# Late modulation in pairs of sections with the ones held in the array, and attention heads whose DVE and PE work is reordered

## The reference

```
m_lat = jnp.split((s_lat @ mod_w[l] + mod_b[l])[:, None, :], 6, axis=-1)   # six sections of 1024 per layer
u = modulate(rmsnorm(h, norm_mix[l]), m_lat[0], m_lat[1])
...
qd = q * exp(b); kd = k * exp(-b); kr = k * exp(b_last - b)     # b: running sum of the log gates in a chunk
o_intra = (mask * (qd @ kd^T)) @ v;   ds = kr^T @ v
s = decay * s + ds                                               # state from chunk to chunk, in both directions
o = o_intra + qd @ s_before
o = o * rsqrt(mean(o*o) + EPS) * gain * silu(g)
hyena: x0 * (fftconv(v * x1) + skip * v * x1), each of x0, x1, v after a 3-tap convolution
```

## Time and profile before

| | us |
|---|---|
| median of 3 timed runs | 2494.81 (2491.34 to 2498.23) |
| profiled execution, its own time | 2485.07 |
| its span | 2483.2 |
| PE busy in the span | 2370.1 (95%) |
| DVE busy | 1147.8 (46%) |
| ACT busy | 363.1 (15%) |
| mean granted clock of TensorE | 0.985 |

### The profile page before, as it was taken

The page is one execution under the profiler, slowest core; times in us unless marked ns, Lnnn a source line. Parts: engine busy times, 40 slices in busy tenths (PEclk is TensorE's granted clock), DMA queues, the critical chain, the costliest instruction groups (busy, mean ns, idle before and its releaser), DMA issues.

```text
span 2483.2 us, 33406 instructions
## 1 busy us (share of the span) xinstructions
PE 2370.1 (95%) x14147; PEld 1038.7 (42%) x14148; DVE 1147.8 (46%) x2426; ACT 363.1 (15%) x654; POOL 293.3 (12%) x313
## 2 busy tenths in 40 slices
PE   7999999989999999999999899999999999999997
PEld 3455445454555533333233344444555333333333
DVE  4677377757845523332222643444454333322226
ACT  3210333321012100000000230000121000000002
POOL 2000000001000212212220000000002212221200
PEclk9999999999999999999999999999999999999999
DMA  9586000120170699999999611113107999999994
GB/s 344 199 284 219 26 26 26 51 77 34 68 296 26 251 376 400 402 395 413 404 411 383 220 35 50 51 34 116 46 34 281 383 405 399 413 403 411 399 377 195
DMA packets 140562, 581.41 MB, mean 234 GB/s; under 512 B 16788, under 2 KB 41672, under 8 KB 87800
## 3 DMA queue, kind: packets, MB, share of 16 engines
q1 hardware_dynamic: 120680, 534.87, 55.3%
q0 software_dynamic: 19648, 44.09, 4.8%
q10 hardware_dynamic: 80, 0.26, 0.0%
HBM read 550.74 MB, written 44.32 MB: 240 GB/s over the span
## 4 chain that ended last, share of the span: by engine, by line
PE 76%; DMA 12%; DVE 10%; issue 1%; ACT 1%; POOL 0%; SPq 0%; DVEq 0%; POOLq 0%
PE ps L1736 23%; PE ps L1896 11%; PE ps L1771 9%; PE ps L1616 9%; DMA arena<-in_ex_w_dram 8%; PE ps L1392 2%; PE ps L1848 2%; PE ps L1360 2%; PE ps L1408 2%; DVE arena L2172 2%; PE ps L1429 2%; DMA arena<-expert_rows 1%; PE ps L1531 1%; PE ps L1550 1%; PE ps L1870 1%
## 5 line engine op out<-in xcount | busy, mean ns | idle before, releaser
L1736 PE MATMUL ps<-arena 128*32 128x512 f32 x6144 | 679.3, 597 | 16.2 <-DMA arena<-in_ex_w_dram 16.1
L1736 PEld LDWEIGHTS ps<-arena 128*32 128x32 f32 x6144 | 198.2, 110 | 449.7 <-issue 448.0
L1771 PE MATMUL ps<-arena 128*32 128x512 f32 x3072 | 340.2, 594 | 12.5 <-DMA arena<-in_ex_w_dram 12.2
L1896 PE MATMUL ps<-arena 128*128 128x512 f32 x616 | 264.5, 592 | 0.0
L2548 DVE TENSOR_TENSOR arena<-arena,ps 128x512 f32<-128x512 f32 x48 | 52.5, 1093 | 456.4 <-PE ps L1736 456.4
L1616 PE MATMUL ps<-arena 128*128 128x512 f32 x512 | 229.4, 598 | 1.6 <-DVE arena L2324 1.6
L1771 PEld LDWEIGHTS ps<-arena 128*32 128x32 f32 x3072 | 106.5, 110 | 238.0 <-issue 238.0
L843 POOL DMA_INDIRECT arena<-normed_rows,arena x184 | 185.2, 1006 | 110.2 <-DVE arena L2566 53.9
L2593 DVE TENSOR_TENSOR arena<-ps,gates 128x512 f32<-128x512 f32 x96 | 61.8, 686 | 258.2 <-PE ps L1771 258.2
L1896 PEld LDWEIGHTS ps<-arena 128*128 128x128 f32 x616 | 117.2, 190 | 147.2 <-issue 147.2
L1429 PE MATMUL ps<-arena 128*128 128x512 f32 x384 | 167.3, 594 | 0.7 <-issue 0.7
(11 more groups left out here) (323 smaller groups left out, 2307.6 us busy)
## 6 DMA issues: line engine op xcount, KB each, us to landing
arena<-in_ex_w_dram SPq DMA_DIRECT2D x384, 1024.0 KB, 11.1
arena<-in_mod_w_dram SPq DMA_DIRECT2D x24, 2048.0 KB, 9.0
arena<-expert_rows SPq DMA_DIRECT2D x16, 1024.0 KB, 7.9
arena<-in_od_w_in_dram SPq DMA_DIRECT2D x12, 1024.0 KB, 5.3
expert_rows<-gates SPq DMA_DIRECT2D x8, 1024.0 KB, 23.1
normed_rows<-arena POOLq DMA_DIRECT2D x16, 512.0 KB, 2.9
arena<-in_ev_w_in_dram SPq DMA_DIRECT2D x3, 2048.0 KB, 18.2
arena<-in_ev_w_in_dram SPq DMA_DIRECT2D x12, 512.0 KB, 4.1
```

The costliest lines, as they stand in the source:

```text
L1736: ins = nc.tensor.matmul(bank(2 + m)[c:c + n], x[:, j, c:c + n], w_slot(e % 2, m, KC, FE)[:, j], start=j == 0, stop=j == KC - 1)
L1771: ins = nc.tensor.matmul(bank(5 + half)[c:c + n], HT[:, j * P + c:j * P + c + n], w_slot(e % 2, 2, FC, D)[:, j, half * 512:(half + 1) * 51 ...
L1896: ins = nc.tensor.matmul(bank(4 * (g % 2) + b), x[:, j], y[:, j], start=first and j == 0, stop=j == 3, skip_group_check=True)
```

## The change

Four sets of edits.

1. Sums over partitions in pairs of sections. `late_columns` goes. `late_rows(q)` holds a 128 x 32 block of ones as weights and streams 512 columns of ACC, four times, each into its own 32 PSUM partitions of bank 7 (two sections of 1024 are four times 512). DVE's `row_in` copies the bank to ACC_ROW, `late_turns(q)` transposes its four 128 x 128 blocks into bank 7, and `columns_in(q)` adds the bias for both sections. There are five calls of each instead of ten of late_columns: late_rows after L1377's group, after s = 2 and 7, n = 1 and 5; late_turns after s = 0, 3 and 8, n = 2 and 6.
2. The last two slabs (18 and 19) go to buffers 1 and 2 instead of 0 and 1, and each is requested when the slab before its predecessor is used up. keep_gates waits for 16 slabs instead of 20.
3. PE in a head: low_rank(h+1) goes to banks 0 to 2 and starts with no wait of its own; the next head's first Hyena piece follows it, ahead of the output's transposes, which use banks 3 and 4. The wait for the MIX writes moves ahead of the key transposes.
4. DVE in a head: conv(h, 1) behind the masked copies; then the first half of gate_logits(h+1) ahead of the mean square, the second half (`gate_magnitudes`) behind it; scaling; then conv(h, 2) and the MIX write, both in head h.

```diff
+        def pairs_read(q):
+            return 1 + 3 * q
+        M_LAST = 2 * NSEC - 2
+        def late_slab(m):
+            return m % 3 if m < M_LAST else m - M_LAST + 1
+        def gate_bank(h):
+            return 0 if h else 2
+        def o_bank(h):
+            return 3 if h + 1 < HEADS else 0
...
-                        sp.wait_ge(m_used, m - 2)
+                        sp.wait_ge(m_used, m - 2 if m < M_LAST else m - 1)
...
-                act.wait_ge(m_used, 2 * NSEC)
+                act.wait_ge(m_used, M_LAST - 2)
...
-            def late_columns(g):
-                pe.wait_ge(m_used, 2 * g + 2)
-                if g:
-                    pe.wait_ge(m_ready, 1 + g)
-                for j in range(KC):
-                    ins = nc.tensor.matmul(bank(7)[:, g * KC + j:g * KC + j + 1], ACC[:, g % 2, j * P:(j + 1) * P],
-                                           cst[:, K_ONE:K_ONE + 1], start=True, stop=True)
+            def late_rows(q):
+                pe.wait_ge(m_used, 4 * (q + 1))
+                pe.wait_ge(m_ready, pairs_read(q))
+                for g in range(4):
+                    ins = nc.tensor.matmul(bank(7)[32 * g:32 * g + 32], cst[:, K_ONE:K_ONE + 32],
+                                           ACC[:, g // 2, (g % 2) * 512:(g % 2 + 1) * 512], start=True, stop=True)
+                ins.then_inc(m_cols, 1)
+            def late_turns(q):
+                pe.wait_ge(m_ready, pairs_read(q) + 1)
+                for c in range(4):
+                    ins = nc.tensor.transpose(bank(7)[:, c * P:(c + 1) * P], ACC_ROW[:, c * P:(c + 1) * P], ident)
                 ins.then_inc(m_cols, 1)
...
-                    if n in (0, 2):
-                        late_columns(8 + n // 2)
-                pe.wait_ge(m_ready, 1 + NSEC)
+                    if n in (1, 5):
+                        late_rows(3 + n // 4)
+                    if n in (2, 6):
+                        late_turns(3 + n // 4)
...
                 if h + 1 < HEADS:
-                    pe.wait_ge(at_ready, 2 * (h + 1))
-                    pe.wait_ge(o_copied, 2 * (h + 1))
                     low_rank(h + 1)
+                    hyena_part(h + 1, 0, 0)
...
+                def row_in(q):
+                    dve.wait_ge(m_cols, 2 * q + 1)
+                    V.tensor_copy(ACC_ROW, bank(7)).then_inc(m_ready, 1)
+                def columns_in(q):
+                    dve.wait_ge(m_cols, 2 * q + 2)
+                    turned = bank(7).rearrange("p (c g r) -> p g c r", g=4, r=32)
+                    for k in range(2):
+                        l, s = SECTIONS[2 * q + k]
+                        V.tensor_tensor(mod[:, l, s].rearrange("p (g c) -> p g c", c=4),
+                                        turned[:, 2 * k:2 * k + 2, :, 0],
+                                        vec_cols[:, :, 6 * l + s].rearrange("p (g c) -> p g c", c=4), ALU.add)\
+                            .then_inc(m_ready, 1)
...
                         if g >= 2:
-                            dve.wait_ge(m_cols, g - 1)
+                            dve.wait_ge(m_cols, 2 * (g // 2) - 1)
...
-                        if g and not half:
-                            columns_in(g - 1)
-                columns_in(NSEC - 1)
+                        if g >= 2 and g % 2 == 0:
+                            (row_in, columns_in)[half](g // 2 - 1)
+                row_in(NSEC // 2 - 1)
+                columns_in(NSEC // 2 - 1)
...
             def gla_head(h):
-                if h:
-                    hyena_conv(h - 1, 2)
...
                 hyena_conv(h, 0)
-                hyena_conv(h, 1)
...
+                hyena_conv(h, 1)
+                if h + 1 < HEADS:
+                    gate_logits(h + 1)
                 dve.wait_ge(o_copied, 2 * (h + 1))
                 V.tensor_scalar(rstd[:, 0:TT], ss[:, 0:TT], 1.0 / DV, EPS, ALU.mult, ALU.add).then_inc(oss_ready, 1)
+                if h + 1 < HEADS:
+                    gate_magnitudes(h + 1)
...
-                if h + 1 < HEADS:
-                    gate_logits(h + 1)
-                else:
-                    hyena_conv(h, 2)
+                hyena_conv(h, 2)
```

More of the change, by code:

```diff
@@ L185, in build @@
         M_SLABS = [at(n, KC, 512) for n in (22528, 31744, 35840)]
-        ACC, ACC_PART = at(39936, 2, D), at(41984, 512)
+        ACC, ACC_PART, ACC_ROW = at(39936, 2, D), at(41984, 512), at(42496, 512)
         X0 = at(31744, TT + CT, D)
@@ L532, in late_modulation @@
                     if m >= 3:
-                        sp.wait_ge(m_used, m - 2)
+                        sp.wait_ge(m_used, m - 2 if m < M_LAST else m - 1)
                     elif m:
                         sp.wait_ge(xn_ready, 4 * m)
-                    sp.dma_start(M_SLABS[m % 3], mod_slab(l, 2 * sec + m % 2)).then_inc(m_full[m % 3], 16)
+                    sp.dma_start(M_SLABS[late_slab(m)], mod_slab(l, 2 * sec + m % 2))\
+                        .then_inc(m_full[late_slab(m)], 16)
             def rows_in():
@@ L796, in gates_out @@
             def gates_out():
-                pool.wait_ge(m_ready, 1 + NSEC)
+                pool.wait_ge(m_ready, pairs_read(NSEC // 2))
                 for l in range(DEPTH):
@@ L1368, in gla_projections @@
                         turned += 1
-                    if i == 6 or i == 9:
-                        late_columns(i // 3 - 2)
                 pe.wait_ge(small_in, SMALL0)
@@ L1379, in gla_projections @@
                     ins.then_inc(r_mm, 1)
+                late_rows(0)
                 slab_in(L0_QK)
@@ L1394, in gla_projections @@
                     ins.then_inc(qk_mm, 1)
-                    if s in (0, 2, 4, 6, 8, 9):
-                        late_columns(2 + (s + 1) // 2)
+                    if s in (2, 7):
+                        late_rows((s + 3) // 5)
+                    if s in (0, 3, 8):
+                        late_turns((s + 1) // 4)
                 pe.wait_ge(r_ready, 3)
@@ L1417, in low_rank @@
                     n = 512 if q < 2 else CTX
-                    nc.tensor.matmul(bank(2 + q)[:, 0:n], w_gate_up[:, h], RT[:, q * 512:q * 512 + n],
+                    nc.tensor.matmul(bank(gate_bank(h) + q)[:, 0:n], w_gate_up[:, h], RT[:, q * 512:q * 512 + n],
                                      start=True, stop=True).then_inc(gx_mm, 1)
@@ L1435, in gla_head @@
                     pe.wait_ge(sg_ready, 2 * HEADS)
-                hyena_part(h, 0, 0)
+                    hyena_part(h, 0, 0)
+                    pe.wait_ge(m_ready, pairs_read(NSEC // 2))
                 hyena_part(h, 0, 1)
@@ L1441, in gla_head @@
                 pe.wait_ge(kr_ready, 3 * h + 1)
+                if h:
+                    pe.wait_ge(omix_ready, 2 * h)
                 for q in range(3):
@@ L1449, in gla_head @@
                 pe.wait_ge(krt_ready, 3 * (h + 1))
-                if h:
-                    pe.wait_ge(omix_ready, 2 * h)
                 for c in range(NCH + NCC):
@@ L1497, in gla_head @@
                     for i in range(4 * half, 4 * half + 4):
-                        ins = nc.tensor.transpose(bank(half)[:, (i % 4) * P:(i % 4 + 1) * P], OT[:, i], ident)
+                        ins = nc.tensor.transpose(bank(o_bank(h) + half)[:, (i % 4) * P:(i % 4 + 1) * P], OT[:, i], ident)
                     ins.then_inc(o_T, 1)
@@ L2073, in late_modulation @@
                         m = 2 * g + half
-                        dve.wait_ge(m_full[m % 3], 16 * (m // 3 + 1))
-                        w = M_SLABS[m % 3]
+                        dve.wait_ge(m_full[late_slab(m)], 16 * (m // 3 + 1))
+                        w = M_SLABS[late_slab(m)]
                         acc = ACC_PART
@@ L2089, in late_modulation @@
                         dve.wait_ge(m_used, 2 * g + half + 1)
-                        if g and not half:
-                            columns_in(g - 1)
-                columns_in(NSEC - 1)
-                dve.wait_ge(m_ready, 1 + NSEC)
+                        if g >= 2 and g % 2 == 0:
+                            (row_in, columns_in)[half](g // 2 - 1)
+                row_in(NSEC // 2 - 1)
+                columns_in(NSEC // 2 - 1)
+                dve.wait_ge(m_ready, pairs_read(NSEC // 2))
                 dve.wait_ge(m_used, 2 * NSEC)
@@ L2107, in gate_logits @@
             def gate_logits(h):
+                if h:
+                    dve.wait_ge(o_mm, 2 * h)
                 for q in range(3):
@@ L2112, in gate_logits, with gate_magnitudes @@
                     dve.wait_ge(gx_mm, 3 * h + q + 1)
-                    V.tensor_scalar(T1[:, cs], bank(2 + q)[:, 0:n], cols[:, R_BA + h:R_BA + h + 1], 0.0,
+                    V.tensor_scalar(T1[:, cs], bank(gate_bank(h) + q)[:, 0:n], cols[:, R_BA + h:R_BA + h + 1], 0.0,
                                     ALU.add, ALU.min).then_inc(gx_read, 1)
+            def gate_magnitudes(h):
                 for q in range(3):
@@ L2118, in gate_logits @@
                     dve.wait_ge(gx_read, 6 * h + 3 + q)
```

(7 more changed lines are left out.)

## The result

| | before | changed |
|---|---|---|
| median, first comparison (4 runs each) | 2493.07 (2482.49 to 2498.23) | 2464.83 (2461.84 to 2467.02) |
| ratio (estimated from all runs, not the quotient of the medians), 95% interval | | 0.9891 [0.9857, 0.9926] |
| median, second comparison (20 and 6 runs) | 2487.07 (2479.37 to 2496.38) | 2462.55 (2461.7 to 2470.79) |
| ratio, 95% interval | | 0.9913 [0.9893, 0.9932] |
| profiled execution, span | 2483.2 | 2465.2 |

The chain by engine on the page of the changed kernel answers to the earlier trace rows: DVE's share falls from 10 to 6%, PE's rises from 76 to 81%.

The account below looks back on a forecast made before the run. The prediction took PE's work and waits to bound the kernel, PE being 76% of the chain. Gains of 7.6 before the heads, 6.2, 5.1 and 1.0 in them sum to 19.9 us: 2494.8 becomes 2474.9, range 2467 to 2486.

Parts of the forecast that it names:

- Base: Whole kernel: the starting time was taken as 2494.8 us, the median of the runs shown, 9.7 above the profiled execution.
- PE up to the last gate piece: From the values through G6: PE is 24 us ahead at low_rank's end (196.9 against 220.9) and reaches 247.2.
- late_rows at 0.9: Late sums: groups of four matmuls run together, so late_rows' eight records cost 0.9 us, 3.4 if nothing overlaps.
- The new wait: Before G7: PE stands 13.5 us for a SiLU that ACT has queued behind decays(0), which waits for DVE's gate logits.
- Its clock: In G7 behind the new wait: PE at half clock for a while, a loss of 3.6 us (bounds 0 and 6.9).
- Rival E: After the stall at G7: PE stays at 1.2 GHz far into head 0, making the kernel slower, 2502; chance 5%.
- State chain: In four heads: DVE's state chain starts 1.6 us earlier, PE's wait falls from 2.1 to 0.5; 6.2 us gained.
- From O to the key transposes: Between heads: the stretch from O's end is 1.7 us shorter, with PE waiting 1.9 for DVE; three times, 5.1 us.
- Clock in the heads: In the products behind PE's waits in two heads: up to 2 us of clock loss could go; 1.0 was taken.
- Slabs: DVE's late loop: some 2 us of wait for the last two slabs, with slab 19 ended at about 235.
- Rival B: Late modulation: the last slabs land late, slab 19 is summed 7.7 us after PE wants it, 2482.6; chance 12%.
- D: At G7: the clock doesn't fall or the stall is shorter, 3.6 and 1 to 3 us more gain, 2469; chance 16%.

Follow-up runs that it names:

- experiment 4: The changed kernel with 24 idle matmuls of 256 columns on PE behind the last late_turns: 2462.72 us, ratio to before 0.9896.
- experiment 7: The kernel before with only hyena_conv(h,1) moved behind the masked copies on DVE: 2481.98 us, ratio 0.9966.
- experiment 5: The changed kernel with each late_rows preceded by the same four sums written to one column group: 2480.82 us.
- experiment 6: The changed kernel with slabs 18 and 19 back in buffers 0 and 1 and keep_gates waiting for all 20 slabs: 2483.26 us, ratio to before 0.998.

## Why the prediction missed its range

Two terms failed: the base from which the gain was taken off, and the size of the gain, in the stall before G7 and in the heads.

- **Base (the step "The median of the runs shown is 9.7 above that one").** This is the larger half of the miss. The 2494.81 of three runs was high: with the 2487 to 2489 of the later comparisons the same 19.9 us give 2467 to 2469. My range held uncertain costs only, and nothing for the base, though its own row had 2491 to 2498 beside a profiled 2485. Why the first three runs were all high stays open: only 9 of the 64 later runs of that kernel in the three comparisons reach 2491.34, the lowest of the three.
- **PE up to the last gate piece:** right, in part by luck: the 0.6 us wait for slab 7 didn't come, and the ten projection pieces took 62.5 us instead of 61.8. low_rank ended at 196.9 as forecast; PE reached the end of late_turns(4) at 248.2 (forecast 247.7).
- **late_rows at 0.9:** 1.0. The Trainium skill's drain at a change of tiling mode (TensorEngine Tiling (Array Packing), section Tiling Modes) has at most 0.14 us for both switches together, the 1.00 less two rounds of 0.43. The pieces ahead of late_rows are no longer than the one ahead of late_turns, where the tile doesn't change (13.87 us for two, 6.97 for one). The trace doesn't contradict the rule, but it has no weight here.
- **The new wait:** place and releaser right, size 11.9 instead of 13.5 (my terms as written add up to 13.2). I set a table load behind the wait for the logits; ACT had done it at 226.63, 26 us early. The row at 252.57 allowed both readings, for ACT had just become free there.
- **Its clock:** 3.6 estimated, 9.23 - 7.0 = 2.2 measured (1.5 to 2.1 by experiment 4; 1.6 to 3.0 over the five profiles with this stall). I took the low time after the restart from two restarts that began with 3 us of late_columns; behind these, at 109.98 and 216.33, PE ran low for 5 and 4 us more, about as long as here. Rival E falls: after 11.9 us idle PE was at full clock inside 264 to 266, four to five us after its restart. The Trainium skill's clock stuck low for over 50 us (TensorE: Matmul & The Clock Gate, section Seeing it yourself) isn't shown by any run here. Together 10.0 us at head 0, not 7.6.
- **State chain:** 6.2 forecast, 6.1 measured (8.4 to 2.3).
- **From O to the key transposes:** 1.7 for a head forecast, 2.0 measured: 5.9 us. I had the MIX writes 0.3 late.
- **Clock in the heads:** I took half of 2 us; with the wait at 0.6 all of it goes (experiment 7). Sum for the heads 14.0, not 12.3.
- **Slabs:** DVE waited 1.1 and 1.5 us for the last two (2 forecast) and ended them at 235.4 (235). Rival B didn't come, D came in part.

So the gain of the change was under-sized by 4.1 us (24.0 at the first residue against 19.9: 2.4 before head 0, 1.7 in the heads), and the base was too high by about 7.

## What to carry to other kernels

When PE is made faster in front of a chain on another engine, ask which instruction in that engine's queue stands ahead of what PE needs next; here one reorder on ACT gave 15 us, more than the 10 that the new sums had kept. Move an off-path vector operation out of the stretch that PE waits behind: more than half of the heads' gain was one convolution moved. And give the base an uncertainty of its own: three runs of a kernel with such a scattering phase didn't fix it to 0.3%.

## What the runs showed of the hardware

How long PE runs at the low clock after a restart isn't fixed by the idle time before it. After the same 11.9 us of idle it was 4.3 us in the changed kernel, 3.1 in its second profile and 5.9 in experiment 5. After 14.3 us, in experiment 6, it was 5.3. After 4.9 us in the kernel before it was 8.3, of which the first 3.4 were late_columns. Matmuls with no use kept the granted clock at 1.00 through a stall in which it fell to 0.50 without them (experiment 4). ACT loaded its table ahead of the wait of the instruction that needs it (226.63 against 254.24). Four 128 x 32 matmuls of 512 columns took 1.0 us in four column groups and 3.4 in one (experiment 5).
